# A decoder step on one Trainium2 core: the experts of tokens 256 to 511 as dense products over all experts

## The reference

```
def peer(x, w_q, sub_keys, expert_u, expert_v):      # x (T, 1024)
    q = (xc @ w_q).reshape(blk, 8, 2, 128)           # 8 heads, two halves
    s = einsum('thcd,hcnd->thcn', q, sub_keys)       # 128 keys for each half
    s1, i1 = top_k(s[:, :, 0], 16); s2, i2 = top_k(s[:, :, 1], 16)
    top_s, top_c = top_k(s1[:, None] + s2[None, :], 16)   # of 256 candidates
    e = i1[top_c // 16] * 128 + i2[top_c % 16]       # expert number, of 16384
    g = softmax(top_s)
    act = gelu(einsum('td,thkd->thk', xc, expert_u[e]))
    return einsum('thk,thkd->td', g * act, expert_v[e])
```

## Time and profile before

| what | value |
|---|---|
| median of 3 runs | 2055.41 us |
| lowest, highest | 2049.02, 2062.79 us |
| span of the profiled execution | 2046.5 us |
| busy share of PE, DVE, ACT, POOL | 76%, 67%, 32%, 38% |
| moved | 771.34 MB, of it 637.59 MB by the queue with the gathers |
| gathers | 520 |

### The profile page before, as it was taken

One profiled execution on the slowest core, in us unless ns is written; L12 is line 12 of the kernel. 1 busy time (PEld: TensorE's weight loads), 2 busy tenths in 40 slices (PEclk: granted clock), 3 DMA queues, 4 the chain that ended last, 5 costly groups with the idle time before them and its releaser, 6 DMA issues. The chain is left out here.

```text
span 2046.5 us, 23894 instructions
## 1 busy us (share of the span) xinstructions
PE 1550.3 (76%) x8074; PEld 727.4 (36%) x8074; DVE 1364.9 (67%) x2605; ACT 664.0 (32%) x1845; POOL 768.3 (38%) x882
## 2 busy tenths in 40 slices
PE   8999889999997776777686667776457558466656
PEld 6647434486463433343321223332112112112112
DVE  1688898984178777566654567777577797545544
ACT  3223245411113354444323223323233423223224
POOL 1232233332534333334334443434334444344441
PEclk9999899999998999889899889888678889788778
DMA  5677998999989999999999999999999999999995
GB/s 190 209 271 239 353 367 319 354 340 365 362 332 416 418 419 418 417 414 415 411 417 420 394 420 419 418 396 421 416 392 411 402 414 421 390 409 417 421 422 226
DMA packets 158011, 771.34 MB, mean 377 GB/s; under 512 B 26888, under 2 KB 27424, under 8 KB 90304
## 3 DMA queue, kind: packets, MB, share of 16 engines
q0 software_dynamic: 103072, 637.59, 77.4%
q1 hardware_dynamic: 54816, 132.22, 17.5%
HBM read 761.50 MB, written 5.58 MB: 375 GB/s over the span
## 5 line engine op out<-in xcount | busy, mean ns | idle before, releaser
L2364 PE MATMUL bank<-arena 64*64 64x512 f32 x4096 | 629.2, 745 | 433.7 <-ACT arena L1257 430.0
L1763 DVE CUSTOM_DVE_ANT_0 arena<-arena 128x1024 f32<-128x1024 f32 x520 | 629.7, 1225 | 458.9 <-DMA arena<-experts_in,arena 454.9
L810 POOL DMA_INDIRECT arena<-experts_in,arena x520 | 577.7, 1111 | 857.1 <-PE bank L2364 749.6
L2364 PEld LDWEIGHTS bank<-arena 64*64 64x64 f32 x4096 | 158.1, 158 | 853.0 <-ACT arena L1257 623.3
L1246 ACT ACTIVATE arena<-arena 128x2 f32<-128x2 f32 x260 | 52.8, 203 | 878.4 <-DVE arena L1763 873.7
L757 POOL DMA_DIRECT2D arena<-cache_k_in x256 | 137.4, 537 | 323.3 <-DVE arena L1349 281.7
L1344 DVE TENSOR_TENSOR arena<-arena 128x2048 f32<-128x2048 f32 x64 | 146.2, 2284 | 15.9 <-DMA arena<-scratch_q 10.6
L1257 ACT ACTIVATE arena<-arena 128x64 f32<-128x64 f32 (+1 forms) x520 | 152.3, 340 | 8.5
L1349 DVE TENSOR_REDUCE arena<-arena 128x32 f32<-128x2048 f32 x64 | 146.2, 2285 | 1.7
L202 DVE TENSOR_TENSOR arena<-arena 128x512 f32<-128x512 f32 (+9 forms) x215 | 130.1, 610 | 12.6 <-DMA arena<-xT_in 7.3
L2276 PE MATMUL bank<-arena 128*128 128x256 f32 (+1 forms) x512 | 127.8, 404 | 6.8 <-DVE arena L202 5.0
(11 more groups left out here) (124 smaller groups left out, 1349.5 us busy)
## 6 DMA issues: line engine op xcount, KB each, us to landing
arena<-cache_k_in POOLq DMA_DIRECT2D x256, 256.0 KB, 5.5
arena<-w_stream_in SPq DMA_DIRECT2D x124, 512.0 KB, 7.8
arena<-cache_v_in SPq DMA_DIRECT2D x160, 256.0 KB, 6.6
arena<-cache_v_in POOLq DMA_DIRECT2D x96, 256.0 KB, 6.7
arena<-experts_in,arena POOLq DMA_INDIRECT x520, 12.8
arena<-xT_in SPq DMA_DIRECT2D x4, 520.0 KB, 5.1
arena<-scratch_q SPq DMA_DIRECT2D x1, 2048.0 KB
arena<-x_rows_in SPq DMA_DIRECT2D x2, 1024.0 KB
```

The lines of the kernel that those rows point to most:

```text
L810: pool.indirect_dma_start(gring[:, s, :], None, A["experts"], bass.IndirectOffsetOnAxis(ap=rows, axis=0)).then_inc(g_landed[s], 16)
L1763: last = V.tensor_tensor_reduce(gring[:, s, 0:D], gring[:, s, 0:D], x_rows, 1.0, 0.0, ALU.mult, ALU.add, dot[:, s:s + 1])
L2364: last = mm(bank[2 * r + c2][out, :], diag[rows, s], gring[rows, s, cols], start=start, stop=True, skip_group_check=True)
```

## The change

Only row tiles 0 and 1 are gathered (`GT = 2`, 64 steps). Row tiles 2 and 3, 256 tokens, multiply *all* 16384 experts in 128 pieces (chunks) of 128 experts.

- Pass 1, its queries, key lists and pair selections are moved into the 64 steps that are left: three weight tiles in a step (steps 10 to 17), two output tiles in a step (19 to 22), one query in each of steps 28 to 43 and its list three steps later, pairs up to step 50.
- For row tiles 2 and 3 no expert numbers are made. In steps 53 to 63 a gate matrix is built: for a token, DVE makes two 128x128 one-hot matrices from its 128 chosen (key 1, key 2, share), PE multiplies them to a 128x128 matrix of shares over all experts, ACT copies four tokens' worth at a time, and SP writes it to device memory (`by_expert`, 8 x 2 MB). In the dense phase SP reads it back in windows of eight chunks, 1 MB each.
- In the dense phase (`for i in range(CHUNKS)`): SP loads the expert_u rows of the chunk in four DMAs of 32 partitions x 4 x 256 floats, DVE transposes them in 32x32 blocks (STREAM_TRANSPOSE), PE makes the 128x256 scores in 8 matmuls, ACT takes the GELU, DVE multiplies by the window of the gate matrix, and PE, two chunks later (`LAG`), multiplies by the expert_v rows, which POOL loads, in 4 matmuls of 128x512.
- The samples' selection, gathers and end, and the ple part of row tiles 0 and 1 are done beside the chunks (`beside`); row tiles 2 and 3 end together after the last chunk.

```diff
-QUERIES_AT = ({-1: 9, 0: 10, 1: 11, 3: 12, 4: 13, 5: 14, 6: 15},
-              {g: j for j, g in enumerate((49, 50, 51, 52, 55, 56, 57, 58, 61, 62, 63, 64, 67, 68, 69, 70))})
...
+GT = 2
+QUERIES_AT = ({-1: 9, 0: 10, 1: 11, 3: 12, 4: 13, 5: 14, 6: 15}, {28 + j: j for j in range(16)})
...
+RB_AT, GATES_AT, WO_AT = 7, 10, 19
+XP_AT, TURN_AT, BUILD_AT, BUILD_EACH = 46, 51, 53, 6
...
+RING_U, RING_C, RING_GS, LAG, AHEAD, WINDOW = 3, 6, 6, 2, 2, 8
...
+            def load_pieces(n):
+                if n >= RING_U:
+                    sp.wait_ge(u_turned, n - RING_U + 1)
+                else:
+                    sp.wait_ge(pq_ready, 32)
+                for q in range(4):
+                    sp.dma_start(raw_ring[n % RING_U][BLOCK * q:BLOCK * q + BLOCK],
+                                 A["experts"][P * n:P * n + P, chunk(q)].rearrange("(a b) r -> b a r", a=4)).then_inc(u_in[n % RING_U], 16)
...
+            def window(w):
+                if w >= 2:
+                    sp.wait_ge(s_gated, WINDOW * (w - 1))
+                else:
+                    sp.wait_ge(g_used, 4 + GATHERED)
+                sp.dma_start(windows[w % 2].rearrange("p (b n) -> p b n", b=DENSE_TOKENS // TB),
+                             by_expert[:, :, TB * WINDOW * w:TB * WINDOW * w + TB * WINDOW].rearrange("b p n -> p b n")).then_inc(window_in[w % 2], 16)
...
+            def gelu(i):
+                act.wait_ge(s_made, i + 1)
+                if i >= RING_GS:
+                    act.wait_ge(c_used, i - RING_GS + 1)
+                A_(gs[:, i % RING_GS], bank[6 + i % 2][:, 0:DENSE_TOKENS], ACT.Gelu).then_inc(s_gelu, 1)
...
+            def build(n):
+                if n % (P // GROUP) == 0:
+                    dve.wait_ge(built_taken, n // (P // GROUP) + 1)
+                if n >= 2:
+                    dve.wait_ge(built, 2 + n - 1)
+                for j in range(GROUP):
+                    at = GROUP * n + j
+                    key_1, key_2, share = (by_slot[:, u, at:at + 1] for u in range(3))
+                    V.tensor_scalar(hot[:, n % 2, 0, j], cst("iota"), key_2, None, ALU.is_equal)
+                    last = V.tensor_scalar(hot[:, n % 2, 1, j], cst("iota"), key_1, share, ALU.is_equal, ALU.mult)
+                last.then_inc(hot_ready, 1)
...
+            def turn_pieces(i):
+                dve.wait_ge(u_in[i % RING_U], pieces_in + 64 * (i // RING_U + 1))
+                if i < RING_U:
+                    dve.wait_ge(g_used, GATHERED + 1)
+                else:
+                    dve.wait_ge(s_made, i - RING_U + 1)
+                V.transpose(turned[i % RING_U].rearrange("p k (a b) -> p k a b", a=4),
+                            raw_ring[i % RING_U].rearrange("p a (k f) -> p k a f", k=KD)).then_inc(u_turned, 1)
...
+            def gate_chunk(i):
+                if i % WINDOW == 0:
+                    dve.wait_ge(window_in[i // WINDOW % 2], x_in + 16 * (i // WINDOW // 2 + 1))
+                dve.wait_ge(s_gelu, i + 1)
+                by_block = gs[:, i % RING_GS].rearrange("p (b t) -> p b t", t=TB)
+                share = windows[i // WINDOW % 2].rearrange("p (b c t) -> p b c t", c=WINDOW, t=TB)[:, :, i % WINDOW]
+                V.tensor_tensor(by_block, by_block, share, ALU.mult).then_inc(s_gated, 1)
...
+            def build(n):
+                if n == 0:
+                    pe.wait_ge(pq_taken, 32)
+                pe.wait_ge(hot_ready, n + 1)
+                if n >= 2:
+                    pe.wait_ge(built_taken, 2 + n - 1)
+                for j in range(GROUP):
+                    last = mm(bank[4 + n % 2][:, j * P:j * P + P], hot[:, n % 2, 0, j], hot[:, n % 2, 1, j], start=True, stop=True)
+                last.then_inc(built, 1)
...
+            def chunk_scores(i):
+                pe.wait_ge(u_turned, i + 1)
+                if i >= 2:
+                    pe.wait_ge(s_gelu, i - 1)
+                else:
+                    pe.wait_ge(built_taken, 2)
+                for k in range(KD):
+                    last = mm(bank[6 + i % 2][:, 0:DENSE_TOKENS], turned[i % RING_U][:, k], xp[:, k],
+                              start=(k == 0), stop=(k == KD - 1))
+                last.then_inc(s_made, 1)
+
+            def chunk_values(i, t):
+                pe.wait_ge(s_gated, i + 1)
+                pe.wait_ge(chunk_in[i % RING_C], pages_in[i % RING_C] + 16 * (i // RING_C + 1))
+                for c2, b in enumerate(ROW_BANKS[t]):
+                    last = mm(bank[b][:, :], gs[:, i % RING_GS, t * P:t * P + P], value_ring[i % RING_C][:, 512 * c2:512 * c2 + 512],
+                              start=(i == 0), stop=(i == CHUNKS - 1))
+                return last
+
+            for i in range(CHUNKS):
+                chunk_scores(i)
+                if i == LAG:
+                    pe.wait_ge(h2_ready, GT)
+                if i >= LAG:
+                    chunk_values(i - LAG, 0)
+                    chunk_values(i - LAG, 1).then_inc(c_used, 1)
+                beside(i)
```

More of the change, by code:

```diff
@@ L261, in build @@
         assert end_back4 <= end4 <= COLS, (end_back4, end4)
-        tail, end_tail = lay(kept["wring"][0], [("ple_w", 2 * D), ("xn3T", D)])
-        assert end_tail <= kept["wring"][1]
+        tail, end_tail = lay(back4["gring"][0], [(f"turned{n}", D) for n in range(RING_U)] + [(f"values{n}", D) for n in range(RING_C)] + [("xn3T", D)])
+        assert end_tail <= back4["gring"][0] + 10 * D
         maps = {}
@@ new lines, in builds, with slot_weights @@
+            def builds(g):
+                if g == XP_AT:
+                    order_pieces(2)
+                    order_pieces(3)
+                    take_pieces(2)
+                    take_pieces(3)
+                elif g == TURN_AT:
+                    take_slots(2)
+                    take_slots(3)
+                first = BUILD_EACH * (g - BUILD_AT)
+                for n in range(max(0, first), min(GROUPS, first + BUILD_EACH)):
+                    take_built(n)
+            def slot_weights(n, two, weights, rows, mask):
+                act.wait_ge(dots, n)
+                A_(act_g[:, two], dot[:, two], ACT.Gelu).then_inc(gated, 1)
+                act.wait_ge(gated, 2 * n - 1)
+                for s in range(two.start, two.stop):
+                    last = A_(coef[:, s:s + 1], weights[s - two.start], ACT.Copy, scale=act_g[:, s:s + 1])
@@ L1252, in slot_weights @@
                 last.then_inc(gated, 1)
-                act.wait_ge(gated, n)
+                act.wait_ge(gated, 2 * n)
                 act.wait_ge(g_used, n)
-                for s in (2 * g, 2 * g + 1):
-                    rows, mask = (diag[:, s, 0:NB], cst("sample_of")) if samples else (diag[:, s], cst("ident64"))
-                    last = A_(rows, mask, ACT.Copy, scale=coef[:, s:s + 1])
+                for s in range(two.start, two.stop):
+                    last = A_(rows[s - two.start], mask, ACT.Copy, scale=coef[:, s:s + 1])
@@ L1263, in _ @@
                     pass_work(now)
-                    embeddings(now)
                     selection(now)
+                    builds(now)
                     i = step // 2
@@ L1614, in select_end @@
                 flat = lambda x: x.rearrange("p h k -> p (h k)")
-                c.also(V.scalar_tensor_tensor, out=expert[0:R, t, slots], in0=flat(top[0:R, 7, heads]), scalar=float(NKEYS),
-                       in1=flat(top[0:R, 8, heads]), op0=ALU.mult, op1=ALU.add)
+                if t not in (2, 3):
+                    c.also(V.scalar_tensor_tensor, out=expert[0:R, t, slots], in0=flat(top[0:R, 7, heads]), scalar=float(NKEYS),
+                           in1=flat(top[0:R, 8, heads]), op0=ALU.mult, op1=ALU.add)
                 dve.wait_ge(*exped)
@@ new lines, in embed_half, with root_of @@
+            def embed_half(t, c2, rows, sums, done=None):
+                cols = slice(512 * c2, 512 * c2 + 512)
+                dve.wait_ge(ple_sig, 1 + 2 * t + c2 + 1)
+                c.also(V.tensor_tensor, rows[:, cols], rows[:, cols], sums, ALU.mult, signal=sum_taken if done is None else None)
+                c.then(V.tensor_tensor, h1row(t)[:, cols], h1row(t)[:, cols], rows[:, cols], ALU.add,
+                       signal=y_out if done or c2 else None)
+            def root_of(t):
+                c.also(V.reciprocal, rstd2[:, 5 + t:6 + t], ssq[:, 5 + t:6 + t], signal=xn3_ready)
@@ new lines, in _ @@
+            for i in range(CHUNKS):
+                if i + AHEAD < CHUNKS:
+                    turn_pieces(i + AHEAD)
+                gate_chunk(i)
+                beside(i)
+            for t in range(2, NT):
+                dve.wait_ge(c_used, CHUNKS - LAG + t - 1)
+                row = xn2A[:, t - 2]
+                for c2, b in enumerate(ROW_BANKS[t - 2]):
+                    cols = slice(512 * c2, 512 * c2 + 512)
+                    c.then(V.tensor_tensor, h1row(t)[:, cols], h1row(t)[:, cols], bank[b], ALU.add, signal=h2_ready if c2 else None)
```

(11 more changed lines are left out.)

836 lines of the change are left out of this document (456 added, 380 removed).

## The result

The changed kernel takes 2460.12 us (median of 4 runs, 2456.95 to 2461.35), the kernel before 2052.22 beside it: **ratio 1.199, 95% interval 1.195 to 1.204**, slower by 408 us. The forecast was 1945 us, the range 1900 to 2010. The profiled execution took 2460.24 us with a span of 2458.6.

The account below looks back on a forecast made before the run. DMA transfers were taken to bound the kernel before. Gather phase with last expert matmuls to 1416, plus 9, 483 for the dense phase and 26 for the tail gave 1934; with 8.9 outside the span, 1945 us, range 1900 to 2010.

Parts of the forecast that it names:

- (d): Into the dense phase: 9 us until the first gated chunk, waiting for the gate matrix's first window and queued value pieces.
- (e): Dense phase, 128 chunks: PE sets 3.50 us a chunk, with 40 us of work beside, 483 us in all.
- Rival C: Dense phase: the 32x32 block transpose costs four times the estimate, DVE bounds at 5.4 us a chunk; 2153 us, chance 0.04.
- D: Rival, no change: PE's clock stays at 0.80 in the dense phase, 4.3 us a chunk; 2055 us, chance 0.03.
- Rival A: Dense phase: the pieces' 32-partition DMAs run at half rate and bound a chunk at 4.1 us; 1987 us, chance 0.24.
- (a): Gather phase, steps 0 to 34: 15 more weight tiles cost 19 us, slot 140's dot product at 1025 us.
- (b): Gather phase, steps 35 to 52: DVE sets the pace with dot products, lists and pair selections, 210 us.
- (c): Gather phase, steps 53 to 63, building the gate matrix: DVE sets the pace, 163 us together.
- the 15 us that I had added for hand-overs: Gather phase: allowance for steps in which PE, ACT and DVE wait on one another with three weight tiles a step.
- Rival B: Gather phase squeezed harder: one-hots at 0.27 us and 1 us hand-overs in steps 10 to 52; 2029 us, chance 0.13.
- (f): Tail after the last expert matmuls: two row tiles end together, 26 us with hand-overs, against 35 before.
- The forecast's 8.9 us around the span: Outside the profiled span: the median of runs lay 8.9 us over it and this was taken to remain.

Follow-up runs that it names:

- high_wide_short: high_both with each expert_u piece loaded in four DMAs over all 128 partitions, 1 KB runs, features in another order: 2037.0 us, ratio 0.992.
- high_both: The changed kernel with all operands of the dense phase's score and value products read as bfloat16 (upper 16 bits): 2154.5 us, ratio 1.048.
- gather_high: The changed kernel with the gather phase's row, gate, up, wo and query products read as bfloat16 (upper 16 bits): 2410.5 us, ratio 1.177.

## Why the prediction was wrong

The span came 525 us over the sum of 1934: 448 in (d) and (e), 68 in the gather phase, 9 in the tail.

- **(e), the step that failed.** "Sixteen 128x512 ran in 7.13 us": these sixteen are records, that is eight products. The price was right for a record and half of what a product costs: 8 x 0.43 + 4 x 0.86 = 6.9 us, not 3.44. 128 x (6.90 - 3.50) = 435 us of the 448; the rest is the work beside the chunks, whose matmuls doubled too: PE was busy for 937 us from the first scores to the last values, of which 128 x 6.90 = 883 are the chunks, so 54 beside them, against the 40 taken (the row below). With the right price the forecast would have been a dense phase of over 900 us against the 718 that it replaces, and the sign would have been right.

```profile
1484.70:2423.70 939.00, 937.30 (x3338) 604.57 (x3335) 261.06 (x397) 88.09 (x190) 72.51 (x130) 1.00 0.61 175
```

- What stood around it held: transpose 1.24 us (taken 1.2), gate product 0.43, clock 1.00, no wait for pieces at this pace (14.7 us in all), first transposes right behind the last dot product. Rival C is refuted by the transpose's row, D by the clock.
- **Rival A** was a right mechanism behind another bound. It cannot show at 6.9 us a chunk; with TensorE out of the way it cost 117 us (high_wide_short against high_both), more than the 42 that A had put on it, because the engines' share was then full.
- **(a)** took 453 us from slot 0 to slot 140 where before took 393 and I had allowed 19 more. I counted the extra tiles' DMA time alone. Three tiles a step also bring 24 products = 48 records to PE, which was busy for 115 of 118 us there. TensorE explains 26 of the 41 us missed (gather_high against after); the other 15 are transfers: I had added 7.9 MB at 417 GB/s, and gather_high, with its engines full, moved 10 MB more than before at 407.
- **(b)** held: 213 us, from slot 140 to the first one-hot at 1291.2, for 210, with DVE busy for 193 of them.
- **(c)** 189, from there to 1480.5, for 163. A one-hot pair costs 0.45 us for the 0.38 taken: 256 x 0.07 = 18 us more DVE. The wait for a build of the step before was 21.3 us in all (group L1839), 14 taken; these two are 25 of the 26 missed. One such wait, of 1.98 us, is in the chain, and its reason is PE in the rows' products of the step before (32 records, 5.4 us):

```profile
1341.99 5.36 PE bank L2472 x32
1347.35 1.10 PE bank L2607 x8
...
1348.48 0.33 DVE arena L1839
```

- (a), (b) and (c) miss by 41 + 3 + 26, with 12 in the front; the 15 us that I had added for hand-overs take the sum back to 67 of the 68. Rival B's direction was right, its reason only in part: its one-hots at 0.27 us were 0.225, and what (a) lost were TensorE's records and transfers, not hand-overs.
- **(f)** 35 us after the last expert product, 26 predicted: the two tiles' 32 products took 28 us, not 14.

```profile
2424.82 14.01 PE L2517 MATMUL bank<-arena 128*128 128x512 f32 x32 [0.25 <-ACT arena L200]
...
2439.95 14.00 PE L2517 MATMUL bank<-arena 128*128 128x512 f32 x32 [0.25 <-ACT arena L200]
```

- The forecast's 8.9 us around the span were wrong as well: 1.6 us lie there (2460.24 against 2458.6).

## What to carry to other kernels

Before a duration is multiplied by a count from the source, count the rows of that line against the loops of the program; here one division (512 records / 256 products) would have turned the forecast round. For a chain of equal instructions take the distance between starts, not the mean length of one. Before two milestones are subtracted, look which work stands between them. A dense product in place of a gather pays for every expert and token: compare its passes with the transfer time it frees first, then look at what bounds once the passes are cheap, here DMAs into 32 partitions.

## What was not expected of the hardware

- Twelve fp32 products of a chunk run in 6.90 us of TensorE and the bfloat16 ones in 1.88 at the same clock of 1.00, although the operands were read with a stride of two from fp32 memory.
- Four DMAs of 128 KB that each fill 32 partitions held the engines at a share of 0.98 with 261 GB/s; the same bytes and runs over 128 partitions gave 324. The order 0, 2, 1, 3 won 39 us, the halves on two queues none.
- An SP DMA whose source is split as four feature quarters of 32 rows took 1.93 us to issue, the mean of 32 in a row, and made the kernel 393 us slower than the usual shape. Why it is so slow was not tried.
- The gather phase's first dot product came between 613 and 625 us in these traces, also among kernels whose front is the same (613.6 in gather_high, 625.4 in after). Nothing here explains that.
